# Two transformer blocks in one program: the differential stage's second norm on VectorE, its strips' steps re-spaced, its last gate strip put first

## The reference, cut to what matters

```python
def _diff_layer(x, pos, norm_g, w_in, w_out, q_norm, k_norm, lq1, lk1, lq2, lk2, subln, lambda_init):
    h = _rms(x, norm_g)
    q, k, v, g = jnp.split(h @ w_in, ...)              # 1024 columns each; 8 heads of 2 x 64 for q and k, of 128 for v
    qs = [_rope_partial(_rms(q[:, :, :, c], q_norm), pos) for c in range(2)]
    ks = [_rope_partial(_rms(k[:, :, :, c], k_norm), pos) for c in range(2)]
    lam = exp(sum(lq1 * lk1)) - exp(sum(lq2 * lk2)) + lambda_init
    o = _diff_attention(qs[0], qs[1], ks[0], ks[1], v, lam)   # softmax(q1 k1) - lam * softmax(q2 k2), causal, times v
    o = _rms(o, subln) * (1.0 - lambda_init)
    return x + (o.reshape(b, s, DA_V) * jax.nn.silu(g)) @ w_out
```

## Time and profile before

| | |
|---|---|
| median of 3 runs | 2913.24 us (2910.73 to 2915.46) |
| the profiled execution: its time, its span | 2911.05 us, 2909.2 us |
| TensorE busy | 2843.3 us, 98% |
| VectorE busy | 1676.3 us, 58% |
| ScalarE busy | 1092.2 us, 38% |
| GpSimd busy | 397.3 us, 14% |

### The profile page before, as it was taken

The page is one execution under the profiler, slowest core; times in us unless marked ns, Lnnn a source line. Parts: engine busy times, 40 slices in busy tenths (PEclk is TensorE's granted clock), DMA queues, the critical chain, the costliest instruction groups (busy, mean ns, idle before and its releaser), DMA issues.

```text
span 2909.2 us, 34967 instructions
## 1 busy us (share of the span) xinstructions
PE 2843.3 (98%) x14241; PEld 2363.5 (81%) x14241; DVE 1676.3 (58%) x2400; ACT 1092.2 (38%) x1699; POOL 397.3 (14%) x263
## 2 busy tenths in 40 slices
PE   8999999999999999999999999999999899899988
PEld 7888887888888888888887889888888787678777
DVE  5554357675464533555247776555533677768884
ACT  4322244554332322323234454422222444444442
POOL 2000111110100001000011220100001322154430
PEclk9999999999999999999999999999999999999999
DMA  4332332243233233332323233233323222131211
GB/s 141 101 95 94 95 88 73 66 127 106 87 94 97 88 101 98 101 95 87 105 71 92 68 108 118 80 109 95 101 91 98 70 64 69 47 88 59 72 59 51
DMA packets 302240, 258.08 MB, mean 89 GB/s; under 512 B 11367, under 2 KB 299904, under 8 KB 302080
## 3 DMA queue, kind: packets, MB, share of 16 engines
q1 hardware_dynamic: 300704, 254.76, 28.7%
q10 hardware_dynamic: 1024, 1.05, 0.2%
q0 software_dynamic: 352, 0.03, 0.0%
HBM read 252.66 MB, written 2.10 MB: 88 GB/s over the span
## 4 chain that ended last, share of the span: by engine, by line
PE 82%; DVE 10%; ACT 3%; issue 3%; POOL 2%; DMA 1%; ACTq 0%; SPq 0%; POOLq 0%; DVEq 0%
PE PS L1525 26%; PE PS L1527 25%; PE PS L1526 25%; DVE WL L2255 3%; PE PS L1531 2%; PE PS L1770 1%; DVE AF L2701 1%; DVE SM L2619 1%; ACT AF L2129 0%; PE PS L1623 0%; PE PS L1812 0%; PE PS L1811 0%; DVE AR L2711 0%; ACT WH L1872 0%; POOL SM L2869 0%
## 5 line engine op out<-in xcount | busy, mean ns | idle before, releaser
L2255 DVE TENSOR_TENSOR WL<-RAW,WH 128x1024 fp32r<-128x1024 f32 x480 | 617.9, 1293 | 572.9 <-ACT WH L1872 572.6
L1525 PE MATMUL PS<-XH,WL 128*128 128x512 f32 x2256 | 904.4, 401 | 2.9 <-DVE XL L2265 2.9
L1527 PE MATMUL PS<-XH,WH 128*128 128x512 f32 x2256 | 883.3, 392 | 0.0
L1526 PE MATMUL PS<-XL,WH 128*128 128x512 f32 x2256 | 882.1, 391 | 0.0
L1872 ACT ACTIVATE WH<-RAW 128x1024 fp32r<-128x1024 f32 x448 | 465.4, 1044 | 1005.9 <-PE PS L1527 994.6
L1525 PEld LDWEIGHTS PS<-XH,WL 128*128 128x128 f32 x2256 | 425.8, 189 | 101.5 <-issue 12.7
L1527 PEld LDWEIGHTS PS<-XH,WH 128*128 128x128 f32 x2256 | 425.2, 188 | 91.5
L1526 PEld LDWEIGHTS PS<-XL,WH 128*128 128x128 f32 x2256 | 426.3, 189 | 81.1
L1525 PE MATMUL PS<-AR,WL 128*128 128x512 f32 (+1 forms) x1216 | 465.3, 383 | 7.3 <-DVE SC L2599 3.5
L1527 PE MATMUL PS<-AR,WH 128*128 128x512 f32 (+1 forms) x1216 | 460.7, 379 | 0.0
L1526 PE MATMUL PS<-AR,WH 128*128 128x512 f32 (+1 forms) x1216 | 460.6, 379 | 0.0
(11 more groups left out here) (259 smaller groups left out, 3000.0 us busy)
## 6 DMA issues: line engine op xcount, KB each, us to landing
RAW<-in_w_ffn_gu_dram SPq DMA_DIRECT2D x176, 512.0 KB, 3.5
RAW<-in_w_ffn_down_dram SPq DMA_DIRECT2D x80, 512.0 KB, 3.4
RAW<-in_w_mix_in_dram SPq DMA_DIRECT2D x48, 512.0 KB, 4.0
RAW<-in_w_xkv_dram SPq DMA_DIRECT2D x32, 512.0 KB, 3.4
RAW<-in_a_w_in_dram SPq DMA_DIRECT2D x32, 512.0 KB, 4.2
RAW<-in_w_mix_out_dram SPq DMA_DIRECT2D x16, 512.0 KB, 3.4
RAW<-in_w_xq_dram SPq DMA_DIRECT2D x16, 512.0 KB, 4.1
RAW<-in_w_xo_dram SPq DMA_DIRECT2D x16, 512.0 KB, 3.4
```

The source lines that it names most:

```text
L1525: pe.matmul(o, ll, rh, start=start, stop=False, skip_group_check=skip)
L1526: pe.matmul(o, lh, rl, start=False, stop=False, skip_group_check=skip)
L1527: return pe.matmul(o, lh, rh, start=False, stop=stop, skip_group_check=skip)
L2255: dve.tensor_tensor(l, raw_slot(n), F(h), ALU.subtract).then_inc(sg["wl"].up(n))
```

## The change

- `sq2`'s additions move from GpSimd's queue to VectorE's, between VectorE's part of `norm_a` and what follows.
- `shape_up`: `dn` goes from 7 to 8 ticks. For k, `dsin` goes from 13 to 11 and is now called ahead of `dkb` (12, as before); `dkt` goes from 15 to 16, `dad` from 18 to 17, `dlo` from 22 to 21. For q, `dsin` goes from 13 to 11, `dad` from 18 to 14, `dlo` from 22 to 17.
- `values_of`: `dob` goes from 9 to 10, `dot` from 11 to 15, `dom` from 14 to 17, `dol` from 19 to 22.
- `opening`: gate strip g7 comes ahead of the two output tiles, and `own_banks(2, 3)` behind it; the unit of g7 is loaded ahead of theirs.

```diff
--- before.py
+++ after.py
@@ -238,9 +238,9 @@
                 def two(k):
                     self.unit(((s, "o01"), k), wo[k * 128:k * 128 + 256, 0:512].rearrange("(k p) c -> p k c", p=128))
 
+                self.strip((s, "g7"), w, 3 * D + 7 * 128)
                 four(0)
                 two(4)
-                self.strip((s, "g7"), w, 3 * D + 7 * 128)
                 four(1)
                 two(6)
                 for p in (2, 3):
@@ -809,15 +809,18 @@
             k = w, t
             self.due("dlo", (w, t - 1))
             self.add("dsq", k, "dsq", "dg")
-            self.later(7, "dn", k, "dn", "dm", "df")
             self.later(3, "swap", k, "dr")
+            self.later(8, "dn", k, "dn", "dm", "df")
             if w == "k":
+                self.later(11, "dsin", k, "dsn", "dco")
                 self.later(12, "dkb", k, "dkb")
-            self.later(13, "dsin", k, "dsn", "dco")
-            if w == "k":
-                self.later(15, "dkt", k, "dkt")
-            self.later(18, "dad", k, "dad", *(("dkm",) if w == "k" else ()), "eh")
-            self.later(22, "dlo", k, "el")
+                self.later(16, "dkt", k, "dkt")
+                self.later(17, "dad", k, "dad", "dkm", "eh")
+                self.later(21, "dlo", k, "el")
+            else:
+                self.later(11, "dsin", k, "dsn", "dco")
+                self.later(14, "dad", k, "dad", "eh")
+                self.later(17, "dlo", k, "el")
 
         def qk(w, t):
             b = self.take()
@@ -841,10 +844,10 @@
             self.add("doq", ("o", t), "doq")
             self.give(b, "dom", ("o", t))
             self.later(4, "don", ("o", t), "don", "dos", "dop")
-            self.later(9, "dob", ("o", t), "dob")
-            self.later(11, "dot", ("o", t), "dot")
-            self.later(14, "dom", ("o", t), "dog", "dov", "oh")
-            self.later(19, "dol", ("o", t), "ol")
+            self.later(10, "dob", ("o", t), "dob")
+            self.later(15, "dot", ("o", t), "dot")
+            self.later(17, "dom", ("o", t), "dog", "dov", "oh")
+            self.later(22, "dol", ("o", t), "ol")
 
         def att(n0, n1):
 
@@ -920,10 +923,10 @@
             self.resid(s, (2 * p, 2 * p + 1), ((out[p], 0), (out[p], 1)))
 
         def opening():
+            yield from gated(7)
             self.own_banks(2, 3)
             for c in range(2):
                 yield from self.tile(out[0], c, c, range(6))
-            yield from gated(7)
 
         def filler():
             for c, b in ((0, 6), (1, self.take())):
@@ -2289,6 +2292,14 @@
                 dve.tensor_copy(S[4].rearrange("p (i w) -> p i w", i=4),
                                 RCOL.unsqueeze(2).to_broadcast([128, 4, 128])).then_inc(sg["rcol2"].up(s))
 
+            def sq2(s, m):
+                if m == 0:
+                    return
+                on.wait_ge(*sg["sq2"].at(s, m))
+                if m > 1:
+                    on.wait_ge(*sg["acc2"].at(s, m - 1))
+                dve.tensor_tensor(S[5], S[5], square2_of(m), ALU.add).then_inc(sg["acc2"].up(s, m))
+
             def xfin(s, m):
                 on.wait_ge(*sg["rb"].at(s))
                 on.wait_ge(*sg["xl"].at(s, m))
@@ -2744,7 +2755,7 @@
                     on.wait_ge(out_done[i], 16)
                 dve.tensor_copy(S[i], PS[OB[p]][:, :]).then_inc(sg["svd"].up(p, hf))
 
-            do = {"setup": setup, "xin": xin, "gains": gains, "tables": tables, "lam": lam, "low": low, "xl": xl, "norm_a": norm_a, "norm2a": norm2a, "xfin": xfin,
+            do = {"setup": setup, "xin": xin, "gains": gains, "tables": tables, "lam": lam, "low": low, "xl": xl, "sq2": sq2, "norm_a": norm_a, "norm2a": norm2a, "xfin": xfin,
                   "barrier": barrier, "resid": resid, "fg": fg, "fu": fu, "fw": fw, "fl": fl, "mq": mq, "xkl": xkl, "xvl": xvl, "xqe": xqe, "xql": xql, "xs": xs, "xn": xn, "xtl": xtl, "evl": evl,
                   "forget": forget, "ctr": ctr, "ms": ms, "mn": mn, "mps": mps, "bps": bps, "mpl": mpl, "xpl": xpl,
                   "cc": cc, "cv0": cv0, "cv1": cv1, "cv2": cv2, "cv3": cv3, "cv4": cv4, "cb0": cb0, "cb1": cb1, "cbl": cbl,
@@ -2804,14 +2815,6 @@
                     on.wait_ge(*sg["acc"].at(s, m - 1))
                 pool.tensor_tensor(S[5], S[5], square_of(m), ALU.add).then_inc(sg["acc"].up(s, m))
 
-            def sq2(s, m):
-                if m == 0:
-                    return
-                on.wait_ge(*sg["sq2"].at(s, m))
-                if m > 1:
-                    on.wait_ge(*sg["acc2"].at(s, m - 1))
-                pool.tensor_tensor(S[5], S[5], square2_of(m), ALU.add).then_inc(sg["acc2"].up(s, m))
-
             def norm_a(s):
                 on.wait_ge(*sg["ms"].at(s))
                 if s:
@@ -2888,7 +2891,7 @@
                 on.wait_ge(*sg["zero"].at(s))
                 pool.tensor_tensor(b, b, OM[n % 2][:, :, T - N + 1:T + 1], ALU.mult).then_inc(sg["gprob"].up(s, n))
 
-            do = {"setup2": setup2, "split": split, "scale": scale, "low": low, "sq": sq, "sq2": sq2, "norm_a": norm_a, "norm2a": norm2a,
+            do = {"setup2": setup2, "split": split, "scale": scale, "low": low, "sq": sq, "norm_a": norm_a, "norm2a": norm2a,
                   "barrier": barrier, "mpq": mpq, "mn": mn, "cb2": cb2, "ny_a": ny_a, "mem_a": mem_a, "dn": dn, "dsin": dsin,
                   "don": don, "bmul": bmul}
             for kind, key in order:
```

## The result

The kernel after takes 2941.07 us (median of 4 runs, 2939.44 to 2944.77), the kernel before beside it 2913.51: a ratio of 1.0098, 95% interval 1.0087 to 1.011. The change costs 27.6 us. The forecast was 2919.2, range 2904 to 2927: the sign was right and the size was not.

The account below looks back on a forecast made before the run. TensorE, busy 98% of the span, was taken as the bound, with 21 us idle in the stage. Terms -2.2 + 12.8 - 4.4 - 3.8 + 3.6 = +6.0 us on the median 2913.24 gave 2919.2, range 2904 to 2927.

Parts of the forecast that it names:

- Strips k: k strips: the sine product's wait for the swap now delays the copy, so TensorE waits at the transposes; +12.8 us.
- the head's part: Stage's head, within the second norm's sum: k0's sine product now stands in front of `dkb`; +0.8 us as an estimate.
- The clock: TensorE in the stage: a new wait over 2 us brings a clock drop, costing 1.7 us beside its length.
- Strips q: q strips: earlier `dsin`, `dad` and `dlo` remove TensorE's waits for `dlo` and a clock drop; -4.4 us.
- Opening: Opening: g7 covers the wait for `dad` of q7, but o6's norm chain and VectorE's score rows cost more; +3.6 us.
- Values' norm: Values' norm: later `dot` leaves some 0.2 of TensorE's 4.0 us wait for `dob`; -3.8 us.
- Second norm: Stage's head: adds on VectorE remove the 1.8 us wait; later `dn`, k0 and half a clock drop also counted; -2.2 us.
- Swaps in time: k strips: every swap takes 4.2 us, strips sum -1.3 for +12.8, total -8.1, 2905.1 us; chance 0.19.
- Absorbed: Stage: waits at `dkt` only replace later ones, half the k strips' sum left, total about -0.4, 2912.8 us; chance 0.22.
- VectorE late everywhere: k2 and k7 collide too, larger opening backlog, clock drops twice there; +11.5, 2924.7 us; chance 0.14.

Follow-up runs that it names:

- d_only_dsin: Kernel before with only a k strip's sine product (`dsin`) moved to 11 ticks, called ahead of the norm copy (`dkb`); 2937.15 us, ratio 1.0085.
- k_dsin_load_held: Kernel before with the k strips' `dsin` at 11 ticks ahead of `dkb`, and SyncE's loads next to k1 to k7 swaps held until landing; 2916.12 us, ratio 1.0015.
- m_q_sum_16: Kernel before with only q strips' spacing changed: `dsin` at 11 ticks, sum (`dad`) at 16, low part (`dlo`) at 19; 2914.1 us, ratio 1.0011.
- e_only_sq2: Kernel before with only the second norm's additions of squares (`sq2`) moved to VectorE; 2911.7 us, ratio 0.9997.
- j_load_held: Kernel before with SyncE's load next to each k swap (k1 to k7) held until the swap has landed; 2909.52 us, ratio 0.9991.
- i_cos_after_copy: Kernel before with k strips' `dsin` at 11 ticks ahead of `dkb`, and GpSimd's cosine product held behind that copy; 2933.85 us, ratio 1.0077.
- n_after_held: Kernel after (whole change) with the loads next to the k strips' swaps held until the swap has landed; 2917.42 us, ratio 1.0026.

## Why the prediction was wrong, by its steps

- **Strips k, +12.8, measured +24.6 alone.** This is the step that failed, in its size: the mechanism (a wait for the swap's landing that now stands ahead of the copy) is what the trace shows in every strip. Of the +12.8, waits were 9.4 and the clock 3.4; in the stretch of d_only_dsin they are 16.6 and 12.1. Three numbers in it were wrong. The copy was taken at 0.43 us, which the earlier trace rows show where it is beside no GpSimd product; behind a common landing it is beside one in k1 to k7, and takes 1.49. The trace of before had this to see: the longest of its eight copies there took 1510 ns, and it is k2's, beside the cosine product of the earlier trace rows, and k7's took 1.50. The transposes were to wait 3.1 + 3.2 + 3.2 us in k1, k3 and k5 and 2.6 more in k4 and k6 together; they wait 24.1 us in all eight. In k2 and k7 the swap was to land in time; in the kernel after the load came 2.0 us behind the first transfer, for 2.44 and 2.66, and collided; that the lateness of TensorE brought it there is an argument, which no run tests. And k0 has 3.7 us for the 0.8 of the head's part: its copy is short, but the operation ahead of it, L2307, took 1.75 us beside GpSimd's product (median of this operation in the kernel before, L2296 there: 0.74).
- **The clock, +0.9 within those sums, measured +15.1.** The argument added a drop at k3 and one at k5 and took one and a half away. In fact there are ten for four, one at every strip, and they last longer, 5.5 us each for the 3.4 read from one: 40.9 us more at the lower level, of which TensorE was idle for a part. That is 15.1 / 6 = 2.5 us for each drop more, for the 1.7 of the forecast. Its rule that a wait of over 2 us brings a drop does not hold everywhere: k_dsin_load_held has three without. (Nor is every one of the four rows that it names over 2 us: the second's longest is 1.5.)
- **Strips q, -4.4, measured +4.3 alone.** Wrong in sign. The waits for `dlo` went as worked out; the earlier sum waits on VectorE for GpSimd, ahead of the score rows, which is a part of it; the rest stays open (m_q_sum_16).
- **Opening, +3.6, measured +8.0 alone.** The chain was right (4.8 forecast, 4.7 and 4.8 measured); the backlog was 3.6 us for 2.3, and a clock drop more came at the chain.
- **Values' norm, -3.8, measured -3.8.** Right in what it did; that the numbers are equal is in part luck.
- **Second norm, -2.2, measured -0.4.** The wait went; 0.8 of the sum was a clock drop by guess, 0.4 was for `dn` a triple later, which e_only_sq2 leaves out, and in the whole change k0's wait stands there.
- **Rivals.** Swaps in time: the hold makes its condition true, 4.0 us each, and the change is then still 6.6 us slower than before, not 8.1 faster: alone, the k strips with the hold are +4.0 for its -1.3, the q strips +4.3 for -4.4 and the opening +8.0 for +3.6. Absorbed: refuted, the waits add to the others and bring the clock down. VectorE late everywhere: nearest, and right that k2 and k7 collide, but its 2924.7 is 16 us short, as it priced the copy and the clock like the forecast.

The Trainium skill (DMA: Bandwidth & Descriptors, Queues, rings and completion order) has it that a DMA engine takes turns between its queues packet by packet, and that a semaphore's write lands only behind that engine's earlier writes, across queues. The swap's times agree: 5.93 us with the load beside it, 4.02 with the load behind it, in the same strip; which of the two it is that holds the swap up, no run tells. The load need not be issued ahead of the last transfer: in k2, k4, k6 and k7 of the kernel after it is issued 2.0 us behind the first, the last transfer 1.98, and the swap takes 5.7 to 6.1 us. The fixed 2 us that the first rival took from the Trainium skill (same page, Anatomy of one DMA) is given there for DMAs that GpSimd issues; the swap's go from ScalarE's queue, and with no load beside them they land 2.0 us behind the last issue (3.99 - 1.98 us).

## What to carry to other kernels

When a wait is moved ahead of other work on an in-order engine, price the work behind it as it runs at the new place: what the same event releases on the other engines may slow it. Count the new waits that are as long as those behind which the clock fell, since each can cost a drop beside its length; and where two events were 0.4 us from colliding, assume that a late engine makes them collide. A small transfer that a step waits for should have the big loads behind it: that is one wait on the loading engine, worth 20.6 us where the step stood in TensorE's way (k_dsin_load_held) and at most a few where it didn't (j_load_held).

## What was not expected of the hardware

- A VectorE copy of 128x512 in SBUF takes 0.43 us alone and 1.49 beside a GpSimd product that began before it, and ends 0.28 us behind that product (k1 to k7 of the kernel after); with the copy first, a VectorE operation on one column took 1.32 us for 0.22. The Trainium skill (SBUF — State Buffer, Who interferes with whom) has it that the two engines share a pair of ports, that whoever issues first keeps it for a whole instruction, and that a copy in SBUF can take it, while an operation with two inputs in SBUF contends with GpSimd's reads; both rows agree. Who is held up can't be read from the starts where they are close: in the k3 rows of after, the sine product, which reads two tiles in SBUF, starts 0.04 us ahead of GpSimd's product and keeps its 0.70 us, and GpSimd's takes 1.77 (1.27 in i_cos_after_copy); in the k2 rows of i_cos_after_copy L2638 also starts 0.04 us ahead of it, and there it is L2638 that is held.
- Four transfers of 8 rows from ScalarE's queue land 4.0 us after the first is issued, with no load beside them, in k1 to k7 of n_after_held, and 5.7 to 6.2 us with one, in k1 to k7 of the kernel after.
